# Reordering the end of an output projection and one store of hidden rows in a one-core decoder layer

## The reference, cut to what matters

```python
    mix = jnp.concatenate([o_a.reshape(Bsz, T, D_A), o_b, o_c], axis=-1)
    x = x + mix @ w_out_l
    hm = rmsnorm(x, g_mlp)
    x = x + jnp.square(jax.nn.relu(hm @ w_up_l)) @ w_down_l
```

## Time and profile before

| | us |
|---|---|
| median of 3 runs | 3059.68 (3055.57 to 3061.14) |
| the profiled execution | 3055.02 |
| its span, first to last instruction | 3053.0 |

### The profile page before, as it was taken

The page is one execution under the profiler, slowest core; times in us unless marked ns, Lnnn a source line. Parts: engine busy times, 40 slices in busy tenths (PEclk is TensorE's granted clock), DMA queues, the critical chain, the costliest instruction groups (busy, mean ns, idle before and its releaser), DMA issues. The chain is left out here.

```text
span 3053.0 us, 50132 instructions
## 1 busy us (share of the span) xinstructions
PE 2866.3 (94%) x20343; PEld 2664.5 (87%) x20343; DVE 2340.3 (77%) x3051; ACT 1151.8 (38%) x1700; POOL 661.5 (22%) x452
## 2 busy tenths in 40 slices
PE   7989999999976888779998999999999999999998
PEld 6948889999865778548887999999999999999998
DVE  6149997996745665478867888898888888888887
ACT  4331222224733111434234555555555333333332
POOL 4543344683521432433320000000000000000000
PEclk9999999999987989779999999999999999999999
DMA  5543334697953000465434566666667865555543
GB/s 191 145 134 98 96 105 136 196 290 225 325 166 128 1 1 1 134 162 155 138 102 148 158 198 191 182 200 188 198 191 266 281 206 193 184 181 202 180 162 107
DMA packets 503491, 499.72 MB, mean 164 GB/s; under 512 B 33898, under 2 KB 439050, under 8 KB 501365
## 3 DMA queue, kind: packets, MB, share of 16 engines
q1 hardware_dynamic: 464400, 423.53, 45.4%
q0 software_dynamic: 12928, 42.02, 3.9%
q10 hardware_dynamic: 25936, 30.98, 2.9%
HBM read 381.13 MB, written 116.52 MB: 163 GB/s over the span
## 5 line engine op out<-in xcount | busy, mean ns | idle before, releaser
L3751 PE MATMUL om_ps<-om_hc,om_ring 128*128 128x272 f32 x5376 | 683.3, 290 | 11.1 <-DVE om_ring L3800 6.4
L3751 PEld LDWEIGHTS om_ps<-om_hc,om_ring 128*128 128x128 f32 x5376 | 682.3, 189 | 12.2 <-DVE om_ring L3800 7.0
L3768 PE MATMUL om_ps<-om_hc,om_ring 128*128 128x272 f32 x5376 | 680.8, 289 | 6.1 <-issue 4.4
L3768 PEld LDWEIGHTS om_ps<-om_hc,om_ring 128*128 128x128 f32 x5376 | 679.6, 189 | 7.4 <-issue 5.7
L3987 ACT ACTIVATE om_ring<-om_late 128x1024 fp32r<-128x1024 f32 x301 | 318.7, 1059 | 387.3 <-PE om_ps L3768 264.8
L3800 DVE TENSOR_TENSOR om_ring<-om_late,om_ring 128x1024 fp32r<-128x1024 f32 x301 | 365.9, 1220 | 79.3 <-ACT om_ring L3987 79.3
L598 PEld LDWEIGHTS pm_ps<-h,w_ring 128*128 128x128 f32 x2688 | 351.3, 190 | 14.7 <-issue 14.6
L598 PE MATMUL pm_ps<-h,w_ring 128*128 128x280 f32 x2688 | 355.9, 294 | 5.1 <-issue 4.1
L538 POOL TENSOR_TENSOR w_ring<-w_raw,w_ring 128x1024 fp32r<-128x1024 f32 (+2 forms) x102 | 233.5, 2311 | 285.7 <-ACT w_ring L641 285.5
L624 PE MATMUL pm_ps<-w_ring,h 128*128 128x512 f32 (+2 forms) x1152 | 238.1, 366 | 2.7 <-PEq L2765 2.7
L3987 ACT ACTIVATE om_ring<-om_raw 128x1024 fp32r<-128x1024 f32 x155 | 164.1, 1059 | 202.2 <-PE om_ps L3768 131.2
(11 more groups left out here) (601 smaller groups left out, 3944.2 us busy)
## 6 DMA issues: line engine op xcount, KB each, us to landing
hid_scratch<-om_x SPq DMA_DIRECT2D x64, 952.0 KB, 7.4
om_hc<-hid_scratch SPq DMA_DIRECT2D x56, 1088.0 KB, 11.8
w_raw<-in_w_in SPq DMA_DIRECT2D x112, 512.0 KB, 3.9
om_late<-in_w_up SPq DMA_DIRECT2D x85, 512.0 KB, 4.9
om_late<-in_w_down SPq DMA_DIRECT2D x85, 512.0 KB, 5.3
om_raw<-in_w_up SPq DMA_DIRECT2D x43, 512.0 KB, 5.0
om_raw<-in_w_down SPq DMA_DIRECT2D x43, 512.0 KB, 5.4
ao_raw<-in_w_out SPq DMA_DIRECT2D x32, 384.0 KB, 4.1
```

What stands on the lines that cost most here:

```text
L3751: last = pe.matmul(ps[:, bank_of(q, idx), 0:HM], f32r(ring[:, n % SLOTS, a, P * k:P * (k + 1)]), f32r(hc[:, c, b, k, :]), start=(idx in (0 ...
L3768: last = pe.matmul(ps[:, bank_of(q, idx) + i, 0:HM], w, f32r(hc[:, slot, b, GJ * half + j, :]), start=(idx in (0, 1, 3) and j == a == b == 0),
```

## The change

In the output stage the last two of eight rounds (`n` of 6 and 7) get another order. On VectorE the low part of piece 8 moves behind `add_tile(12)` to `add_tile(15)`, and the low part of piece 9 behind `plain_lows(7)`; `plain_lows(7)` moves in front of `combos(7)`. On ScalarE the high parts of pieces 8 and 9 move from between the two squares of a round to its end. No instruction is added or removed there.

On SyncE, in step 32, the store of hidden rows 30 moves from behind all seven `load_hidden(0, ...)` to between the third and the fourth of them. The third's place in the order stays.

```diff
@@ in loads(q), SyncE @@
                 load(q, "22")
                 if q == UPS:
-                    for c in MOVES[2:7]:
+                    load_hidden(0, MOVES[2])
+                    store_hidden(q - 2)
+                    for c in MOVES[3:7]:
                         load_hidden(0, c)
@@ in the loop over q, SyncE @@
-                if 2 <= q < UPS + 2:
+                if 2 <= q < UPS + 2 and q != UPS:
                     store_hidden(q - 2)
@@ VectorE, output stage @@
-            for n in range(OUT_PIECES):
+            for n in range(OUT_PIECES - 2):
                 add_tile(2 * n)
                 low(n + 2)
                 add_tile(2 * n + 1)
@@
                     plain_lows(n - 1)
                     combo_lows(n - 1)
                 combos(n)
-            plain_lows(OUT_PIECES - 1)
-            combo_lows(OUT_PIECES - 1)
+            n = OUT_PIECES - 2
+            add_tile(2 * n)
+            add_tile(2 * n + 1)
+            plain_lows(n - 1)
+            combo_lows(n - 1)
+            combos(n)
+            n = OUT_PIECES - 1
+            add_tile(2 * n)
+            add_tile(2 * n + 1)
+            low(piece(0, 0))
+            plain_lows(n - 1)
+            combo_lows(n - 1)
+            plain_lows(n)
+            low(piece(0, 1))
+            combos(n)
+            combo_lows(n)
@@ ScalarE, output stage @@
-            for n in range(OUT_PIECES):
+            for n in range(OUT_PIECES - 2):
                 square(2 * n)
                 high(n + 2)
                 if n:
                     combo_highs(n - 1)
                 square(2 * n + 1)
                 plain_highs(n)
+            for n in (OUT_PIECES - 2, OUT_PIECES - 1):
+                square(2 * n)
+                combo_highs(n - 1)
+                square(2 * n + 1)
+                plain_highs(n)
+                high(n + 2)
             combo_highs(OUT_PIECES - 1)
```

## The result

The changed kernel took 3038.75 us in the median of four executions (3034.55 to 3040.45), the kernel before 3057.62 (3054.82 to 3061.14) in its four; the ratio is 0.9946, with a 95% interval of 0.9923 to 0.9969. The profiled execution took 3039.60, with a span of 3037.6.

A forecast was written before the change was run, and what follows sets the result against it. TensorE was taken to be held up by VectorE's order, the chain behind it and a late store; 5.4 + 2.3 = 7.7 us off 3059.68 gave 3052.0 us, range 3047 to 3058.5.

The forecast's parts named there:

- Bounds of the kernel before: TensorE's idle gaps: 6.41 us before (0,0), 4.23 before (0,2), 4.41 before the late down product, each given a cause.
- S1: First of a step's three sums on VectorE; step 0's was to start at 1661.2 instead of 1666.66, step 33's 1.0 earlier.
- First seam: Between output stage and MLP: the new order starts product (0,2) 5.4 us earlier, bounds 4.2 to 6.7.
- The clock: TensorE's lower level behind the first seam's gaps: a gain of 0 to 1.6 us, taken as 0.
- Second seam: At the first down products: the earlier store starts product (33,2) 2.2 us sooner, 2.3 with the later gap, bounds 1.0 to 3.2.
- the thing named that is late next: At the first down products: step 33's weights, which nothing in the change brings forward, as the queue carries the same bytes.
- Load "22": A weight load; step 33's was to land at 2371.9 as before, letting its first sum run 1.0 us earlier.
- The reload of `x`: Other condition of product (33,2), landed at 2383.2; to move by the queue's dry time, 3.2 us at most.
- Rival (e): Slower: the store's issue held about 9 us delays the fourth load at the first down products; 3062.6 us, chance 0.05.
- the prediction's reading of it: By the rule the store could share the queue with four loads and land near 2366: second seam 0, sum 5.4.
- Sum: Both seams of the kernel together: 5.4 + 2.3 = 7.7 us.
- the one from the profile to the median of the runs: Whole kernel: profiled 3055.02 becomes 3047.3; its 4.7 us below the median carries over, 3052.0; median of three 2 off.

The follow-up runs named there:

- e3_stage_only: Changed kernel with the store of hidden rows 30 back behind all seven loads, so only the output stage's new order; mean 3047.3 us of 12, ratio 0.9982.
- e4_store_only: Kernel before with only the store of hidden rows 30 moved between the third and fourth load; mean 3051.6 us of 12, ratio 0.9992.
- e7_low_in_wait: Changed kernel with the low part of piece 9 moved between `combos(7)` and `combo_lows(7)` on VectorE; mean 3047.5 us, ratio 0.9979.
- e8_low_and_copy: Changed kernel with that low part between `combos(7)` and `combo_lows(7)`, and `copy_out(0,0)` before the square root on ScalarE; mean 3043.0 us of 12, ratio 0.9965.
- e1_after_again: Changed kernel repeated with nothing altered; mean 3047.9 us of 12, ratio 0.9983 against the kernel before.
- e11_store_sixth: Changed kernel with the store of hidden rows 30 between the sixth and seventh load; down products end 683.63 us after product (32,0) starts, no whole time given.

## Why the prediction was wrong

**Bounds of the kernel before: right.** The idle time before (0,0) was VectorE's order, that before (0,2) the chain from S1 through `copy_out(0,0)`, and that before (32,6) the store. e3_stage_only and e4_store_only remove one without the other.

**First seam: right.** In the old trace's time product (0,0) was to start at 1652.8: measured 1646.08 + 6.66 = 1652.74. S1 at 1661.2: 1661.54. Product (0,2) at 1668.6 after 8 us of idle time: 1668.91 after 7.66. 5.4 were forecast, 5.1 came in this pair and 5.0 in the mean of the profiles. The 0.3 are small steps on VectorE that I set too tight: in the old trace's time `low(9)` came 0.1 late, `combos(7)` 0.2 and S1 0.3. e7_low_in_wait and e8_low_and_copy show that the chain was read rightly.

**The clock: as taken.** TensorE ran its first 4 us behind the second gap, from 1662.25, at the lower level of 1.2 GHz, and rose within the half microsecond of this row (stretch, busy, granted clock):

```profile
1666.00:1666.50 0.50, 0.50 (x5) 0.81 0.63 151
```

In the kernel before it stayed there for most of 1674 to 1680. The time at the lower level behind the gap was 3.4 to 5.9 us in the three executions of the changed kernel, and 3.4 and 5.8 in the two of the kernel before. The stretch from (0,2) to (32,0) goes with it, by 1.0 us in the changed kernel and 0.7 in the one before. So 0 was the value to take, with the 0 to 1.6 as a matter of the single execution.

**Second seam: right, with the thing named that is late next.** Store at 2355.3: 2355.2. Fourth load at 2358.0: 2357.9, and the seventh at 2366.1: 2366.1. Load "22" at 2371.9: S1 followed its landing at 2359.49 + 12.69 = 2372.2. Product (33,2) at 2382.0: 2382.1, from e1_after_again, where it started 32.62 behind (32,0). The reload of `x` landed at 2367.8, in the old trace's time 2380.4 instead of 2383.2, and no instruction waits for it any more. 2.3 were forecast, 2.8 came, within 1.0 to 3.2. Of these, 2.1 are there at (33,2), and 0.7 come behind it, which the sum had at 0.1: S1 of step 34 waited 1.83 us for its weights in the kernel before and 0.23 in the changed one. Rival (e) did not come about: the issue of the store took 0.97 us instead of 11.09. With six loads ahead of it, in e11_store_sixth, it took 8.60.

Landings came in the order of issue. The Trainium skill's rule ("DMA: Bandwidth & Descriptors", section "Two DMAs through the same engine are not ordered") gives no such order, and by the prediction's reading of it the seam would have been worth nothing; for transfers of about 1 MB the traces show it all the same, which says nothing on single descriptors.

**Sum: 7.7 forecast, 7.8 at the seams.**

**The step that failed is the one from the profile to the median of the runs, and the range with it.** It said that the median of three runs can stand 2 us off on either side, from runs that spread by 5.6 us. The spread of this program is 28 us over 87 executions, with a standard deviation of 6.7. A median of three or four such executions has a standard error of some 4 us, and a difference of two of them nearly 6: the term was mis-sized by three times. The 4.7 us that the prediction carried over from the profiled execution to the median are such a difference too, and no property of the kernel. The forecast missed the median by 13.3 us. Of these, 7.2 are its starting point: 3059.68 was the median of three executions, where the mean of 87 is 3052.45. Another 5.9 are the result: 3052.45 less the seams' 7.8 is 3044.65, and its four executions had a median of 3038.75. Each lies within two standard errors, but both go the same way, and together they are 2.3 standard errors. That is luck, and rare luck; a cause peculiar to those few executions is not excluded by any run. With 6 us in place of 2 the range would have been some 3043 to 3062, and the result still outside of it; with 12 it would have been 3037 to 3068. The error was to trust either median to 2 us. There was a sign of it in the profile before: a stage in which TensorE works in bursts, at a mean granted clock between its two levels (0.92 from 1000 to 1220). I read only the seams.

The first ratio's interval has the same weakness. It is computed from executions that happened to lie close together, and the later ones put it at 0.9983 and 0.998.

## What to carry to other kernels

Where a change moves less than the spread of single executions, measure it as a distance between two landmarks on either side of the edit, in several profiles: here 0.2 us could be told apart, where the times of 12 executions couldn't tell 3. Before a range is given, the spread of the program must be known from more than three executions, above all if a stage runs at a mean granted clock between its two levels. And when a stall is removed, follow the same queue to what lands next: 4.4 us of a gap were worth 2.8, since the weights behind it came no earlier.

## What the runs showed of the hardware

Two executions of the same instructions can differ by 12 us within a stage of 235 us, with TensorE busy for the same share but granted 0.95 of the clock in one and 0.91 in the other. Behind the same gap of 7.7 us in the same program, TensorE ran at the lower level for 3.4 us in one execution and for 5.9 in another. And one DMA queue under full load delivered stores and loads in the order of issue, so well that landings could be forecast to 0.2 us over 20 us.
